# Issuing the experts' down-weight loads from ScalarE instead of the sync engine

## What is computed

```python
scores = sigmoid(xt @ router_w)                  # 256 tokens x 64 experts
... pick 4 of 8 groups, then 8 experts per token; weights wts
for each expert e, in blocks of its tokens:
    hb = silu(xb @ w_gate[e]) * (xb @ w_up[e])   # 1024 -> 256
    yb = (hb @ w_down[e]) * w                    # 256 -> 1024
routed = sum of the 8 rows of each token
shared = (silu(xt @ ws_gate) * (xt @ ws_up)) @ ws_down
x = layer_norm(ALPHA * x + gate2 * (routed + shared))
```

## Time and profile before

| | before |
|---|---|
| median of 3 runs | 4137.35 us (4134.38 to 4137.35) |
| the profiled execution | 4137.76 us, its span 4136.1 us |
| TensorE busy | 3485.1 us, 84% of the span |
| ScalarE busy | 842.4 us, 20% |
| DMA queue of SP (q1) | 727.16 MB |
| DMA queue of ScalarE (q10) | 2.10 MB |
| experts' stage | 344 to about 990 us, and 1355 to about 2010 us |

### The profile page before, as it was taken

The page is one execution under the profiler, slowest core; times in us unless marked ns, Lnnn a source line. Parts: engine busy times, 40 slices in busy tenths (PEclk is TensorE's granted clock), DMA queues, the critical chain, the costliest instruction groups (busy, mean ns, idle before and its releaser), DMA issues.

```text
span 4136.1 us, 46292 instructions
## 1 busy us (share of the span) xinstructions
PE 3485.1 (84%) x18496; PEld 2414.5 (58%) x18496; DVE 1569.9 (38%) x2703; ACT 842.4 (20%) x1240; POOL 599.4 (14%) x556
## 2 busy tenths in 40 slices
PE   6888999994788899999299958798988994879899
PEld 3754333331566333333098648686978963877688
DVE  4433222224634222222354265531545426554154
ACT  1211111110130111111132221111324223111132
POOL 4402233331440233233100000000000000000000
PEclk8889999997878999999699968779998996877999
DMA  7647999985754899889554300004536430000352
GB/s 264 236 158 279 364 347 354 356 338 197 283 181 168 343 351 353 341 350 358 181 195 153 130 8 1 1 21 147 199 102 225 159 117 21 1 1 13 130 204 102
DMA packets 305420, 799.38 MB, mean 193 GB/s; under 512 B 57030, under 2 KB 155868, under 8 KB 251308
## 3 DMA queue, kind: packets, MB, share of 16 engines
q1 hardware_dynamic: 245804, 727.16, 46.8%
q0 software_dynamic: 58848, 67.05, 4.9%
q10 hardware_dynamic: 544, 2.10, 0.1%
HBM read 989.01 MB, written 53.48 MB: 252 GB/s over the span
## 4 chain that ended last, share of the span: by engine, by line
PE 41%; DVE 6%; ACT 1%; issue 1%; DMA 1%; SPq 0%; DVEq 0%
PE s_bank L1899 12%; PE s_bank L1937 6%; PE s_bank L1887 5%; PE s_bank L2083 2%; PE s_bank L1964 2%; PE s_bank L2098 2%; PE s_bank L2093 1%; PE s_bank L2200 1%; PE s_bank L2210 1%; PE s_bank L2168 1%; PE s_bank L2160 1%; PE s_bank L2071 1%; DMA s_ringA<-in_ffn_in 1%; PE s_bank L2153 1%; PE s_bank L2145 1%
## 5 line engine op out<-in xcount | busy, mean ns | idle before, releaser
L711 PE MATMUL f_bank<-f_ringA,f_arena 128*64 128x512 f32 x3072 | 688.7, 601 | 16.3 <-DMA f_ringA<-in_w_up,f_chosen 10.1
L711 PEld LDWEIGHTS f_bank<-f_ringA,f_arena 128*64 128x64 f32 x3072 | 222.3, 138 | 401.4 <-issue 400.1
L1899 PE MATMUL s_bank<-s_hT_high_parts,s_highA_parts 128*128 128x256 f32 x1408 | 402.7, 286 | 17.7 <-DVE s_hT_parts L2428 17.7
L1899 PE MATMUL s_bank<-s_hT_parts,s_highA_parts 128*128 128x256 f32 x1408 | 402.2, 286 | 0.0
L1899 PE MATMUL s_bank<-s_hT_high_parts,s_ringA_parts 128*128 128x256 f32 x1408 | 402.0, 285 | 0.0
L732 PE MATMUL f_bank<-f_ringB,f_arena 128*64 128x512 f32 x1536 | 346.5, 592 | 1.0 <-DVE f_arena L1473 1.0
L1012 ACT ACTIVATE f_arena<-f_bank 128x512 f32<-128x512 f32 (+1 forms) x362 | 202.1, 587 | 575.1 <-PE f_bank L692 174.2
L1465 DVE TENSOR_TENSOR f_arena<-f_arena,f_bank 128x256 f32<-128x256 f32 x96 | 58.6, 610 | 636.3 <-ACT f_arena L1090 636.3
L1899 PEld LDWEIGHTS s_bank<-s_hT_high_parts,s_highA_parts 128*128 128x128 f32 x1408 | 274.2, 195 | 20.4 <-issue 19.0
L1899 PEld LDWEIGHTS s_bank<-s_hT_parts,s_highA_parts 128*128 128x128 f32 x1408 | 274.3, 195 | 1.4
L1899 PEld LDWEIGHTS s_bank<-s_hT_high_parts,s_ringA_parts 128*128 128x128 f32 x1408 | 274.1, 195 | 0.0
(11 more groups left out here) (393 smaller groups left out, 5361.2 us busy)
## 6 DMA issues: line engine op xcount, KB each, us to landing
f_ringA<-in_w_gate SPq DMA_DIRECT2D x128, 1024.0 KB, 8.7
f_ringA<-in_w_up SPq DMA_DIRECT2D x128, 1024.0 KB, 11.1
f_ringB<-in_w_down SPq DMA_DIRECT2D x128, 1024.0 KB, 12.3
s_ringA<-in_ffn_in SPq DMA_DIRECT2D x88, 1024.0 KB, 7.7
f_ringA<-in_w_ada SPq DMA_DIRECT2D x48, 1024.0 KB, 8.4
s_arena<-in_ffn_out SPq DMA_DIRECT2D x44, 1024.0 KB, 6.0
s_ringA<-in_w_in SPq DMA_DIRECT2D x40, 1024.0 KB, 6.1
f_ringA<-in_w_in SPq DMA_DIRECT2D x28, 1024.0 KB, 10.2
```

Of the source, the lines that this page charges most:

```text
L711: last = mm(ps[j * CAP:(j + 1) * CAP, :].rearrange("p (h c) -> p h c", h=2), picked[:, b % 2, k, j * CAP:(j + 1) * CAP], gu[j][:, :, k, :] ...
L1899: last = mm(ps[:, t * S:(t + 1) * S], parts_of(wx[:, k, cs_]), parts_of(hx[:, k, :]), start=(k == 0 and x == 0), stop=(k == DT - 1 and x = ...
```

## The change

The function `down_rows` moves from SP's program to ScalarE's. SP issues gate and up weights only. ScalarE issues turns 0, 1 and 2 behind the store of `h_rows`, turn 3 behind the first two picked pairs, and in the loop, in iteration b, the down matrices of pair b+1 once it has taken its half of `down(b-1)` out of the bank and the other half of `down(b-1)` is filled. The condition on the slot is the one of before.

```diff
 @block.sync
-                def down_rows(turn, e):
-
-                    if turn == B_SLOTS - 1:
-                        banks.read(sp, ("y", 3))
-                    elif turn >= B_SLOTS:
-                        banks.read(sp, ("down", (turn - B_SLOTS) // 2, 1))
-                    sp.dma_start(slotB(1 + turn), a["w_down"][l, e].rearrange("(p k) c -> p (k c)", p=P)
-                                 ).then_inc(b_landed[(1 + turn) % B_SLOTS], 16)
-
-                for turn in (0, 1, 2):
+                for turn in range(4):
                     gate_up(turn, turn)
-                    down_rows(turn, turn)
-                gate_up(3, 3)
-                for b in range(2, PAIRS + 1):
-                    if b < PAIRS and not spills(b):
+                for b in range(2, PAIRS):
+                    if not spills(b):
                         for j in range(2):
                             gate_up(2 * b + j, columns(b) + j)
-                    if b - 1 >= 1 and not spills(b - 1):
-                        for j in range(2):
-                            if 2 * (b - 1) + j != 2:
-                                down_rows(2 * (b - 1) + j, columns(b - 1) + j)
 @block.scalar
+                def down_rows(b, j):
+
+                    turn = 2 * b + j
+                    act.dma_start(slotB(1 + turn), a["w_down"][l, columns(b) + j].rearrange("(p k) c -> p (k c)", p=P)
+                                  ).then_inc(b_landed[(1 + turn) % B_SLOTS], 16)
...
                               h_rows.rearrange("p m k q -> p m (k q)")).then_inc(h_stored, 16)
+                for b, j in ((0, 0), (0, 1), (1, 0)):
+                    down_rows(b, j)
                 take("router", router[:, 0, :], lambda ps: ps[:, 0:MT * E], ACT.Sigmoid)
...
                     take_picked(b)
+                banks.read(act, ("y", 3))
+                down_rows(1, 1)
...
                         act.nop().then_inc(y_act, 1)
+                        if b + 1 < PAIRS and not spills(b + 1):
+                            banks.read(act, ("down", b - 1, 1))
+                            for j in range(2):
+                                down_rows(b + 1, j)
                     if b + 2 < PAIRS:
                         take_picked(b + 2)
```

## The result

The changed kernel takes 4209.95 us (median of 4 runs, 4201.53 to 4214.96) beside 4136.94 for the kernel before (4134.38 to 4137.35). The ratio is 1.0174, 95% interval 1.0161 to 1.0188: 73 us slower, where 76 had been forecast. One execution of the later kernel e1 took 4674.23 us at a mean granted clock of 0.745 instead of 0.89; it is left out of e1's figures.

A forecast was written before the change was run, and what follows sets the result against it. The experts' stage was taken to run at TensorE's pace. The terms 47 + 12 + 23 − 7 + 1 = 76 us, on 4137.8 us, gave 4214 us (+1.8%); own range 4170 to 4245, wider range 4135 to 4265.

The forecast's parts named there:

- Issue work off SP, 0: On SP, taking away the down issues saves nothing, as no load starts earlier: 0 us.
- issue work on ScalarE, 0: In the loop, the two down issues fit into ScalarE's idle gaps: 0 us.
- The sigmoid, +1: In each layer's head, three issues delay the router's sigmoid by 0.65 us, twice: +1 us, with 0 the other bound.
- The down loads overtake gate and up, +47 and +12: At 30 tight places, queues taking even turns make `up` late: 47 us, plus 12 from the next pair's down loads.
- The second overlap: At the tight places, the next pair's down loads take half from what is left of gate and up: 12 us.
- The clock, +23: TensorE's matmuls slow down behind waits of 2 us or more, at eleven of 30 places, 2.1 us each: +23 us.
- Given back, −7: A later TensorE absorbs 3.7 and 2.9 us of its waits for GpSimd's fetches and slower matmuls: −7 us.
- Hidden loads: Rival, 2 in 10: ScalarE's queue gets under about a third, so gate and up stay within their room; about 4138 us.
- Faster: Rival, under 1 in 10: gate and up land earlier in a layer's first iterations, ending six waits; about 4113 us.
- The dearer one: Rival, 1.5 in 10: already a wait of 1 us lowers TensorE's clock, 63 us instead of 23; about 4254 us.

The follow-up runs named there:

- e1: Changed kernel, but the down loads that met the next pair's gate and up are issued one iteration later, still by ScalarE; 4147.42 us, ratio 1.0027.
- e3: Changed kernel with each down load cut into column halves, moving in pieces of 2 KB instead of 8 KB; 4161.51 us, ratio 1.0061.
- e4: Head of the kernel before; in the loop ScalarE issues gate and up, SP the down loads; 4202.3 us, ratio 1.0161.
- e5: Only the changed kernel's head: turns 0 to 3 on ScalarE, loop down loads on SP as in the kernel before; 4136.11 us, ratio 1.0001.
- e2: Changed kernel, but SP issues the down matrix of a pair's second column behind gate and up, ScalarE the first's; 4139.59 us, ratio 1.0011.
- e6: Unlike the changed kernel, in the loop SP issues gate and, behind it, down, while ScalarE issues up behind its SiLU; 4150.19 us, ratio 1.0029.

## Why the prediction held, step by step

*Issue work off SP, 0; issue work on ScalarE, 0.* Right. ScalarE's gap took the two issues, and e3, with four, has its settled iterations at the old pace. e4 has the waits without the down loads on ScalarE.

*The sigmoid, +1.* The issues were slower (2.44 us for three) and the sigmoid comes 4.35 us after the store's issue instead of 2.3. e5 shows that it costs nothing that can be measured (0.9992 to 1.0010). The term should have been 0, its lower bound.

*The down loads overtake gate and up, +47 and +12.* The mechanism is shown from five sides: taken away (e1), halved (e2), weakened by the size of the pieces (e3), turned round (e4), and two queues without it (e6); and the packets show the even turns directly. The evidence that I gave for sharing was weaker than I thought: in the earlier trace rows the earliest of GpSimd's fetches lands at 393.2 + 9.6 = 402.8, just behind SP's last down load at 402.5, which an order by age would give too. It is the packets of that stretch, shown under e6, that settle it.

The size was too high by a quarter. Forecast were 59 us of new waiting for SP's gate and up; measured are 45.4 (51.5 against 6.1). The two places that I hadn't read, the last of each layer, would by the same reading have 3.0 and 3.9 us instead of 1.4 each, so the full sum would have been further off. Two things made it too high. At the place shown I had gate and up run alone for 3.3 us with 1.3 MB; they ran alone until 556 us with 1.96 MB, because the down loads start to flow some 3.7 us after their issue. So gate and up end together with the down loads (569.3 and 569.4), where by my shares 0.7 to 0.8 MB of them, 1.7 to 1.9 us, were still to come; and when the pair after that sends its own down loads, little is left for them to overtake: in the last 1.4 us before the landing q1 starts only 0.02 MB beside 0.43 of q10. The second overlap, 12 us in the sum, isn't there at this place. The other is the first place of the first layer, where I had the largest delay of all, 4.3 us and a second overlap on top: `up` starts there at 398.43 without a wait. Why it is spared stays open. The settled waits were mostly 0.5 to 1.9 us where I had 0.6 to 4.

*The clock, +23.* Measured +25.4, but with the wrong boundary. I had counted waits from 2 us up. Only 7 of the 34 waits are that long, 3 more than the 4 of the kernel before, and by my own rule they would have given 6 us. Three places of the changed kernel:

```profile
650.50 8.78 PE L696 MATMUL f_bank<-f_ringA,f_arena 128*64 128x512 f32 x32 [0.93 <-DMA f_ringA<-in_w_up]
...
775.56 7.09 PE L696 MATMUL f_bank<-f_ringA,f_arena 128*64 128x512 f32 x32 [1.56 <-DMA f_ringA<-in_w_up]
...
856.64 9.92 PE L696 MATMUL f_bank<-f_ringA,f_arena 128*64 128x512 f32 x32 [1.79 <-DMA f_ringA<-in_w_up]
```

0.93 us is enough at one place and 1.56 us isn't at another. All 7 long waits and 10 of the 27 short ones had slow matmuls behind them, 17 groups against 4 before, each slower by about 2 us. That this term came out, and with it the sum, is luck: the waiting was 14 us less than forecast, and slow matmuls behind waits that I had thought harmless made up for it. Why a wait of one length slows the matmuls here and not there stays open.

*Given back, −7.* The size was near: the waits for GpSimd's fetches fell from 10.1 to 5.7 us, and the slow matmuls behind one of them went too. But the reason that I gave, a TensorE that comes later, fails in the first layer. There `up` of the pair ahead starts at 398.43 where it started at 398.21, no later to speak of. The fetch, issued at 397.04 in both kernels, landed after 11.6 instead of 16.1 us, so the 2.03 us of waiting were gone. Why it landed sooner was not tested.

*The rivals.* Hidden loads would have needed unequal turns, and the packets are nearly equal. Faster would have needed gate loads that stood behind down loads; the two early waits of 2.67 and 3.46 us rose to 4.02 and 4.78 instead. The dearer one, a slow clock behind every wait, was right in part: short waits can do it, but only 10 of 27 did.

*The page of the Trainium skill*, DMA: Bandwidth & Descriptors. Its section "Queues, rings and completion order" has each DMA engine take turns between its queues, packet by packet. The trace agrees, with 201, 210 and 203 packets of three queues in e3. By its section "Issuing engines are not separate DMA queues", issuing from a second engine saves the sequencer's time alone. The trace agrees, with 374 GB/s over the place shown with two queues and 368 with one.

## What to carry to other kernels

One queue served in order is a schedule: the load needed first goes first. Moving the less urgent loads to a second queue gave them equal turns here and took them from the urgent ones, though nobody had waited to issue. Before such a move, compare the room of the urgent load (need minus landing) with the bytes that may pass it at the full rate. A second full queue also thins out a third one, as GpSimd's fetches showed (one turn in three instead of in two), and a wait of one or two microseconds on TensorE can cost as much again in clock (10 of 27 did).

## What was unexpected of the hardware

The size of the pieces sets the share: with pieces of 2 KB against 8 KB, the small ones' queue moved 0.38 MB beside 1.50, stopped delaying the other (at settled places one wait of 0.8 us was left) and kept TensorE waiting up to 17.5 us where three queues were full. The down loads moved their first bytes only 3.25 to 3.75 us after their issue into an empty queue, from ScalarE and from SP alike; why is open. And 50.5 us of useless matmuls, put where TensorE would have been idle, made a kernel 16 us faster.
